# A hybrid decoder step: the sample's attention cut into nine pieces and laid between the prompt's attention steps, four state buffers, and the first part's recurrence laid between attention steps

## The reference

```python
n1 = rmsnorm(x, norm1_g); proj = n1 @ w_in          # q/k/v of both branches, gates
oa = banded_swa(qa, ka, va, sinks)                  # prompt: window 128, 16 heads, 4 kv heads
#  sample: one query per sequence against 127 cached keys and the new one (swa_sink_attend)
log_a = log_sigmoid(zb @ w_gla_gate + b) / 16
og, S_new = gla_recurrent(qg, kg, vg, log_a, S0)    # 4 heads, state 128 x 256 per head
og = rmsnorm(og, gla_norm_g) * silu(rb)
x = x + (sigmoid(ga) * oa + sigmoid(gb) * og) @ w_out
x = x + peer(rmsnorm(x, norm2_g))                   # below
...
def peer(h):   # per token: 8 heads x 16 picked experts of 16384
    ue = take(peer_u, eidx); act = gelu(ue . h); ve = take(peer_v, eidx)
    return sum(g * act * ve)
```

## Time and profile before

| | us |
|---|---|
| median of 3 runs (3849.88 to 3872.11) | 3852.84 |
| profiled execution, its own time | 3859.83 |
| its span in the trace | 3858.0 |
| PE busy | 2894.0 (75%) |
| DVE busy | 2808.5 (73%) |
| POOL busy | 2443.4 (63%) |
| ACT busy | 731.2 (19%) |
| first gather issued at | 484.80 |

### The profile page before, as it was taken

One profiled execution on the slowest core, in us unless ns is written; L12 is line 12 of the kernel. 1 busy time (PEld: TensorE's weight loads), 2 busy tenths in 40 slices (PEclk: granted clock), 3 DMA queues, 4 the chain that ended last, 5 costly groups with the idle time before them and its releaser, 6 DMA issues.

```text
span 3858.0 us, 33048 instructions
## 1 busy us (share of the span) xinstructions
PE 2894.0 (75%) x10008; PEld 1798.1 (47%) x10008; DVE 2808.5 (73%) x5630; ACT 731.2 (19%) x1677; POOL 2443.4 (63%) x2076
## 2 busy tenths in 40 slices
PE   8778689888687997887988768878777555555555
PEld 6667566456563665443664345545654111111111
DVE  0461797887788865866879897887879866667675
ACT  1321013332111131322111102322111110001001
POOL 0000077787667755765766777778667777777776
PEclk9889889899898997898999889989899777676677
DMA  4115399999999988898999999999999999999998
GB/s 149 54 36 183 110 376 407 350 356 396 420 403 345 405 331 324 306 328 309 396 402 375 326 363 403 401 328 370 421 411 380 338 371 368 363 377 385 367 400 336
DMA packets 342240, 1298.82 MB, mean 337 GB/s; under 512 B 39480, under 2 KB 48720, under 8 KB 321936
## 3 DMA queue, kind: packets, MB, share of 16 engines
q0 software_dynamic: 297216, 1082.26, 73.6%
q1 hardware_dynamic: 44848, 214.44, 14.3%
HBM read 1278.87 MB, written 19.76 MB: 337 GB/s over the span
## 4 chain that ended last, share of the span: by engine, by line
POOL 36%; PE 21%; DVE 14%; DMA 13%; issue 12%; DVEq 2%; ACT 0%; ACTq 0%; SPq 0%; POOLq 0%
POOL ringb L569 36%; DMA ringb<-in_v,eidx 9%; PE bank L834 8%; PE vsum L746 4%; DVE ringb L1294 4%; PE bank L1011 3%; DVE acc L1336 2%; PE bank L873 2%; PE bank L888 1%; DVE scT L1691 1%; PE bank L913 1%; DMA arena<-in_s 1%; DMA out_ss<-arena 1%; DMA ringb<-in_u,eidx 1%; DVE idx L1492 1%
## 5 line engine op out<-in xcount | busy, mean ns | idle before, releaser
L569 POOL DMA_INDIRECT ringb<-in_u,eidx x1024 | 1241.6, 1212 | 993.8 <-DVE eidx L1402 482.2
L746 PE MATMUL vsum<-ringb,diag 128*128 128x512 f32 x2160 | 1284.5, 737 | 646.6 <-DMA ringb<-in_v,eidx 603.8
L569 POOL DMA_INDIRECT ringb<-in_v,eidx x1024 | 1181.8, 1154 | 400.6 <-issue 300.1
L1294 DVE CUSTOM_DVE_ANT_0 ringb<-ringb,n2t 128x1024 f32<-128x1024 f32 x1032 | 1234.8, 1224 | 164.7 <-DMA ringb<-in_u,eidx 99.5
L746 PEld LDWEIGHTS vsum<-ringb,diag 128*128 128x128 f32 x2160 | 459.8, 228 | 1352.8 <-issue 1202.1
L1336 DVE SCALAR_TENSOR_TENSOR acc<-ringb,wgt,acc 128x1024 f32<-128x1024 f32 x484 | 622.3, 1286 | 326.0 <-DMA ringb<-in_v,eidx 313.7
L834 PE MATMUL bank<-wring,nTb 128*128 128x256 f32 x3024 | 683.4, 386 | 34.9 <-DMA wring<-in_w 31.1
L834 PEld LDWEIGHTS bank<-wring,nTb 128*128 128x128 f32 x3024 | 546.0, 182 | 175.5 <-DMA wring<-in_w 36.1
L1049 ACT ACTIVATE diag<-cst,wgt 128x128 f32<-128x128 f32 x540 | 206.9, 397 | 863.5 <-PE vsum L746 707.2
L873 PE MATMUL bank<-nTb,wring 128*128 128x256 f32 (+1 forms) x1152 | 264.0, 388 | 6.7 <-DMA wring<-in_w 4.1
L873 PEld LDWEIGHTS bank<-nTb,wring 128*128 128x128 f32 x1152 | 223.9, 195 | 60.6 <-issue 20.7
(11 more groups left out here) (231 smaller groups left out, 2212.5 us busy)
## 6 DMA issues: line engine op xcount, KB each, us to landing
wring<-in_w SPq DMA_DIRECT2D x152, 1024.0 KB, 7.8
ringb<-in_u,eidx POOLq DMA_INDIRECT x1024, 6.5
ringb<-in_v,eidx POOLq DMA_INDIRECT x1024, 6.6
n2t<-scratch_n SPq DMA_DIRECT2D x16, 512.0 KB, 7.4
oab<-in_xp SPq DMA_DIRECT2D x4, 1024.0 KB, 6.9
bTb<-in_keysT SPq DMA_DIRECT2D x4, 1024.0 KB, 9.1
vgb<-in_xp SPq DMA_DIRECT2D x4, 1024.0 KB, 8.9
scratch_h<-vgb SPq DMA_DIRECT2D x4, 1024.0 KB
```

Of the source, the lines that this page charges most:

```text
L569: pool.indirect_dma_start(out=ring[r], out_offset=None, in_=a["u"] if kind == "u" else a["v"], in_offset=bass.IndirectOffsetOnAxis(ap=at, ...
L746: last = mm(out[:, g * 512:(g + 1) * 512], lhs, ring[r][:, g * 512:(g + 1) * 512], start=(x == first), stop=(x == end))
L1294: v.tensor_tensor_reduce(out=ring[r], in0=ring[r], in1=n2t[:, n % 2, :], scale=1.0, scalar=0.0, op0=ALU.mult, op1=ALU.add, accum_out=dg[:, ...
```

## The change

Three things are changed.

First, part 0 takes its steps in another order (`mixer_order`): gate scores first, then attention steps with the recurrence's factors and units between them, and the four `ga` units at the end. For that the recurrence's buffers of part 0 move from `arena` into `ringb`, which no gather uses yet (`recurrence_room`).

Second, the sample's attention in part 2 becomes nine pieces (`sat`, 0 to 8), one after each attention step from 1 on; its evacuations count on a semaphore of their own (`sat`). Its scratch tiles move into `scT`, `kdTok` and `E0b`, and `vS` into `bTb`, where the cached keys are until the scores are made. So the values and the two window copies are issued after weight unit `vb` 3, once the scores are done, no longer after attention. The weights of the marks change: attention's points in part 2 weigh 13 for 10, and the four points of 16 each of the sample's attention are gone.

Third, the sample's states get four buffers (`S0 = 4`): SP issues four loads at once, and a buffer's store and reload follow three states later.

```diff
+def mixer_order(c):
+    NQ = 4 * CH[c]
+    at, A, B = [("at", n) for n in range(NQ + 2)], [("factors", n) ...], [("gla", n) ...]
+    if c == SC:
+        at = [at[0]] + [x for n in range(1, NQ + 2) for x in (at[n], ("sat", n - 1))]
+    if c or CH[c] != 2:
+        return at + [("between", 0), ("gate", 0), ("gate", 1)] + [x for pair in zip(A, B) for x in pair]
+    return [("gate", 0), at[0], at[1], ("gate", 1), at[2], A[0], at[3], B[0], at[4], A[1], at[5], B[1], at[6], A[2], at[7], B[2],
+            A[3], at[8], B[3], at[9]] + [("ga", u) for u in range(4)] + [("between", 0)]
...
-    out += [(("at", n, i), tokens(10) if i == 0 and n % CH[c] == 0 else 10) for n in range(4 * CH[c] + 2) for i in range(2)]
-    out += [(("sat", i), 16) for i in range(4)] if s else []
+    out += [(("at", n, i), (tokens(10) if i == 0 and n % CH[c] == 0 else 10) + 3 * s) for n in range(4 * CH[c] + 2) for i in range(2)]
...
+        def recurrence_room(c):
+            a0 = ringb if together(c) else arena
+            gates0 = 5 * D if together(c) else 0
...
-        SsT, Ps, PsT = (arena[:, 8 * CM + i * P:8 * CM + (i + 1) * P] for i in range(3))
+        SsT, Ps, PsT = scT[:, 0, :], kdTok[:, 0, :], E0b[:, 0:P]
-        vS = Pbb[:, :].rearrange("p (b c) -> p b c", b=NS)
+        vS = bTb[:, 0:2048].rearrange("p (b c) -> p b c", b=NS)
-        evac = {... for e in ("act", "dve")}
+        evac = {... for e in ("act", "dve", "sat")}
...
-                    if c == SC and (kind, u) == ("ga", 1):
-                        quads(MARKS[c][("sat", 0)])
+                    if c == SC and (kind, u) == ("vb", 3):
                         emptied(sp, ("va", c, 0, ST))
-                        sp.wait_ge(p_ready.sem, p_ready.at((c, 4 * CH[c] - 1)))
-                        sp.wait_ge(full.sem, full.at(("PT", c, 4 * CH[c] - 1, 1)))
+                        sp.wait_ge(full.sem, full.at(("sS",)))
                         sp.dma_start(vS[:, :, :], a["vcs"]).then_inc(d_vS, 16)
                         sp.wait_ge(d_vS, 16)
...
                         for b in range(NS):
-                            quads(MARKS[c][("sgla", b)])
-                            if b >= 2:
-                                sp.wait_ge(full.sem, full.at(("ogS", b - 2, 1)))
-                                sp.dma_start(o["ss"][b - 2]..., s0[b % 2]).then_inc(d_st[b % 2], 16)
-                                sp.wait_ge(d_st[b % 2], 16 * (b // 2))
-                            sp.dma_start(s0[b % 2], a["s0"][b]...).then_inc(d_s0[b % 2], 16)
+                            if b >= S0:
+                                quads(MARKS[c][("sgla", b - S0 + 1)])
+                                sp.wait_ge(full.sem, full.at(("ogS", b - S0, 1)))
+                                sp.dma_start(o["ss"][b - S0]..., s0[b % S0]).then_inc(d_st[b % S0], 16)
+                                sp.wait_ge(d_st[b % S0], 16 * (b // S0))
+                            sp.dma_start(s0[b % S0], a["s0"][b]...).then_inc(d_s0[b % S0], 16)
...
-        def pe_sample_attention(pe, beside):
+        def pe_sample_attention(pe, i):
+            if i == 0: # wait for the new keys; 64 score products (sS)
+            if i == 2: # turn SsT (sST)
+            if i == 4: # wait for the softmax; turn Ps (sPT)
+            if i == 6: # wait for vS; 64 products with the values (sO)
+            if i == 8: # 16 turns (sOt)
...
-                    if n == NQ - 1 and c == SC:
+                    if n == 0 and c == SC:
                         sample_operands()
+                    if n >= 2 and c == SC:
+                        dve_sample_attention(dve, n - 1)
                     beside("at", n, 1)
...
+                for what, n in mixer_order(c):
+                    if what == "at":
+                        attention(n)
+                    if what == "sat":
+                        pe_sample_attention(pe, n)
+                    if what == "between":
+                        between()
+                    if (what, n) == ("gate", 0):
+                        gate_scores()
+                    if what == "gla":
+                        recurrence(n)
+                    if what == "ga":
+                        unit(c, "ga", n)
```

More of the change, by code:

```diff
@@ L464, in build @@
         d_vS = sem("d_vS")
[L465 removed]
+        d_s0 = [sem(f"d_s0{i}") for i in range(S0)]
         d_keys = sem("d_keys")
@@ new lines, in pe_sample_attention @@
+            if i == 0:
+                pe.wait_ge(knew, 1)
+                ps = room(pe, ("sS",))
+                for half in range(2):
+                    lo = half * 64
+                    for b in range(NS):
+                        for Q in range(2):
+                            q = 2 * Q + half
+                            last = mm(ps[:, b * HA + q * 4:b * HA + q * 4 + 4], kTs[lo:lo + 64, Q, b, :], fmS[lo:lo + 64, 4 * Q:4 * Q + 4, b],
+                                      start=True, stop=True)
+                    if half == 0:
+                        pe.drain()
+                last.then_inc(full.sem, full.did(("sS",)))
@@ L878, in pe_program, with attention @@
                 emptied(pe, ("fm", c, 9))
-                for n in range(NQ + 2):
+                def attention(n):
                     beside("at", n, 0)
@@ new lines, in gate_scores @@
+                def gate_scores():
+                    beside("gate", 0)
+                    pe.wait_ge(d_par, 80)
+                    emptied(pe, ("fm", c, 18))
+                    for h in range(HB):
+                        ps = room(pe, ("gate", c, h))
+                        mm(ps[:, 0:CT], wg[:, h * DK:(h + 1) * DK], zbT[:, 0:CT], start=True, stop=True)\
+                            .then_inc(full.sem, full.did(("gate", c, h)))
+                    if c == SC:
+                        ps = room(pe, ("gateS",))
+                        for h in range(HB):
+                            last = mm(ps[:, h * NS:(h + 1) * NS], wg[:, h * DK:(h + 1) * DK], fmS[0:RANK, 18, :], start=True, stop=True)
+                        last.then_inc(full.sem, full.did(("gateS",)))
@@ L1207, in decays, with recurrence @@
                     act.sem_inc(e_ready.sem, e_ready.did((c, n)))
-                beside("gla", 0, 0)
-                decays(0)
-                for n, (h, t0, nt) in enumerate(units):
+                def recurrence(n):
+                    h, t0, nt = units[n]
+                    if n == 0 and not together(c):
+                        beside("gla", 0, 0)
+                        decays(0)
                     beside("gla", n, 2)
@@ L1226, in act_program @@
                         decays(n + 1)
-                    if ga_after(c, n) is not None:
+                    if ga_after(c, n) is not None and not together(c):
                         for p in pair_jobs(c):
                             sigmoid("ga", c, ga_after(c, n), p)
+                for what, n in mixer_order(c):
+                    if what == "at" and n <= NQ:
+                        attention(n)
+                    if (what, n) == ("sat", 3):
+                        sample_softmax()
+                    if (what, n) == ("gate", 0):
+                        gate_scores()
+                    if (what, n) == ("gate", 1) and together(c):
+                        decays(0)
+                    if what == "gla":
+                        recurrence(n)
+                    if what == "ga":
+                        for p in pair_jobs(c):
+                            sigmoid("ga", c, n, p)
                 if c == SC:
@@ L1703, in dve_program @@
                     beside("gla", n, 5)
+                for what, n in mixer_order(c):
+                    if what == "at":
+                        attention(n)
+                    if what == "between":
+                        between()
+                    if (what, n) == ("gate", 0):
+                        gate_scores()
+                    if (what, n) == ("gate", 1):
+                        cumulate()
+                    if what == "factors":
+                        factors(n)
+                    if what == "gla":
+                        recurrence(n)
+                    if what == "ga":
+                        branch_gate(n)
                 if c == NCH - 1:
```

393 lines of the change are left out of this document (195 added, 198 removed).

## The result

The changed kernel took 3805.61 us (median of 4 runs, 3796.31 to 3816.66) beside 3862.48 for the kernel before (4 runs, 3849.88 to 3881.05): ratio 0.9884, 95% interval 0.9844 to 0.9925, faster by 29 to 60 us. The forecast was 3809, that is 44 us off the 3852.84 that the kernel before had then. The profiled execution of the changed kernel took 3796.31 itself, the lowest of its four, span 3794.4, 63.6 less than the span before.

What follows compares the result with a forecast made beforehand. From about 482 us the DMA engines' gathers bound the kernel, before that part 0's chain through the mixer. Savings of 17 + 20 + 7 = 44 us took 3859.8 to 3815.8, and 7.0 lower on the median's scale to 3809; range 3790 to 3835.

Steps and rivals of the forecast that it cites:

- Part 0: Part 0's new order of the same instructions: 25.6 us saved, less 9 for the low clock, about 17.
- where before `rb` begins at 279: End of part 0 in the kernel before, set against 253.4 in the new order: 25.6 us saved.
- The 9 us charged for the clock: Part 0: PE's low clock behind waits for DVE's sums, 3 us for each of three cycles.
- The sample's attention: Part 2's attention with the sample's attention in pieces: stretch of 181 us becomes 161, 20 saved.
- Both needs close to it will not dovetail perfectly, and I take 161: Part 2's attention stretch: PE needs 144 us, the DMA engines 157 at best; 161 taken.
- a DMA share of 0.95 and no wait of PE over 6 us: Expected sign in part 2, from attention's first step to the gate scores, with a length of about 161 us.
- The states: The sample's states with four loads in flight: 7 us saved, bounds 0 and 8.
- at 0.98 it is 83: The sample's states: DMA engines' need of 91 x 0.89 = 81 us becomes 83 at a share of 0.98.
- PE as the bound in part 2's attention (3824): Rival for part 2's attention: the stretch takes 176 us and saves 5, total 3824 us; chance 0.18.
- The low clock through part 0: Rival for part 0's new order: 10 us lost there, 27 kept from part 2, 3836 us; chance 0.08.
- The slower case: Rival: low clock in part 2's attention, mean below about 0.75, 20 us slower, 3873 us; chance 0.04.
- if the clock drops in either interleaved stretch: Sign that the forecast is wrong: PE's clock drops in part 0's new order or part 2's attention with the pieces.

Runs made afterwards that it cites:

- the second run with late copies: The changed kernel with part 0's first `ga` unit ahead of its last recurrence unit and the window copies at the second `wo` unit: 3861.27 us, 0.9968 beside the changed kernel.

## Why the prediction was right

The time came 3.4 us below the forecast, and the gain of 44 is what three timings show (45, 50 and 42 by their ratios). The two terms that the runs can resolve, part 0 and the buffers, are there. But the sizes of the terms were off both ways and made each other good: that the sum came out is in part luck.

**Part 0**: forecast 17, measured 24.3 (23.3 in the run that undoes it). The schedule was right: `ga` was to start at 225 + 9 = 234 and starts at 234.42. The step that failed is "where before `rb` begins at 279": the row of PE that starts at 278.74 has 288 products, nine units, and its first is the last `ga` unit; `rb` begins at 286, 7 us later. So the gain is 286 less 262.3 (234.4 + 27.8), 24. The 9 us charged for the clock came in sum, and that is luck, for they were not where I put them: 5.6 are in the head, where the first masks start at 139.9 for 134.3; two cycles take 31.0 and 30.5 for 30.1; and about 3 are in the tail, where the scores of the last unit stand behind the wait of 8.41 at the lower clock. In the head only a part is a wait's (again S takes 3.78 behind a wait of 2.27, as in the earlier trace rows); the gate scores begin at 96.87, not 95, and the first `vb` unit takes 8.86 for 7.17 with no wait before it. The forecast "3 us for each of three cycles" was refuted: behind the wait the products lose about 1.2 us a cycle, and S and the `vb` unit nothing. Here the Trainium skill, "TensorE: Matmul & The Clock Gate", section "HAM oscillation — how this bites in real kernels", has short bursts between waits start cold every time. With that the trace agrees: the products right behind each wait are slow (1.19 for 0.59). That "every cycle would be paid at the low clock" went beyond that, and it did not come: S and the unit 5 us later are at the upper clock (1.99, 7.17).

**The sample's attention**: forecast 20, the stretch gained 13.6, and by the run that undoes the pieces 7 are kept at the end in the mean, with an interval from -4 to 19: the 20 is refuted, a gain is not shown. Two steps failed. "Both needs close to it will not dovetail perfectly, and I take 161" left out that the copies now stand in the middle of attention: "part of the delay hides" was too hopeful, since a gather of 17.38 us stopped PE for 5.33 (9.30 before) and put the next 13 us at the lower clock; without them the stretch is 162, and 164.5 in the second run with late copies. And the term took a shorter stretch for time won, though one quad had left it. The need of PE, 144, was right (144.0 and 147.8 in the two runs with late copies). The sign "a DMA share of 0.95 and no wait of PE over 6 us" was half met: 0.89, and 5.33.

**The states**: forecast 7 with bounds 0 and 8, measured 19.7 in the stage; the run with two buffers puts the buffers at 11.7 in the stage and 11 to 29 us in the time. The other 6 (96.2 before, 90.3 in that run) lie between single executions; their cause stays open. The step that failed is "at 0.98 it is 83": it reckoned the DMA engines' need by their busy share, and took the mean share of a long stretch for a ceiling. The same rows give it by bytes: 91 us at 316 GB/s are 28.8 MB, and at the 378 GB/s of the last of the earlier trace rows they take 76 us. In this stage the share is now 1.01 and the rate 380 GB/s, before 0.89 and 319: each busy us moved fewer bytes before, so the share alone understated what was left. The window was short too, 91 us for a stage of 96.2. That the loads in flight, not SP's wait for the stores, set the pace was right in kind, and the stage's 90.3, 84.9 and 76.5 to 78.6 us with two, three and four buffers show it step by step.

**Rivals.** PE as the bound in part 2's attention (3824) is half true: PE was busy 154.8 of 169 us, and the stretch took between the forecast's 161 and that rival's 176; and the cause was the late `v` tile behind the copies, which that rival had named. The low clock through part 0 did not come (0.85 in the mean). The slower case needed a mean clock below 0.75 in the stretch; it was 0.86. That "a gain of part 2 comes back as DMA idle time in the recurrence behind it" did not come either: that stage took 174.4 for 174.8, with one quad more in it. One sign of a wrong forecast did come: "if the clock drops in either interleaved stretch". It dropped in both, behind the waits of part 0 and twice in part 2, at the 64 score products and behind the copies, where the kernel before had 0.97 up to 1480. So the time was met although a condition of the reasoning was not.

## What to carry to other kernels

Before a stage's length is compared, count the gathered work in it: where marks shift work between stages, a stage can be 16 us shorter because four quads have left it, which says nothing of the kernel's time. A large copy that nothing waits for belongs where the engine that it delays has slack. Work added to test an idle engine must end before the wait does, or it hides what it should show. And an average share over a long stretch is no ceiling for a short one (bytes over the best rate seen come nearer), nor is the start of a row of products that of its last group: read the count of the row.

## What the runs showed of the hardware

The clock fell while TensorE was never idle. The windows of the changed kernel around the 64 score products (64x4 each, from 1360.83 without a gap):

```profile
1362.00:1364.00 2.00, 2.00 (x18) 2.00 (x19) 1.87 (x5) 1.95 (x3) 1.70 (x2) 0.93 0.93 363
1364.00:1376.00 12.00, 11.92 (x43) 9.75 (x44) 5.47 (x8) 4.39 (x13) 4.24 (x4) 0.50 0.72 289
```

The first 24 took 0.9 us for each eight, all later ones 1.7 to 1.8, with the sums of gathered tiles behind them at 6.23 for 3.65. It is the same in all twelve traces with the pieces: the clock falls 1.7 to 4.9 us behind the start of this row. In the kernel before, which has the same attention step there without the row, the clock is 1.00 up to 1378, falls only behind a wait of 5.04 us, and is 1.00 again from 1400 to 1480. So it is likely the long row of tiny products that brings the lower clock, much as waiting does; it is not proven, since PE also waited 1.36 to 2.57 us some 5 us ahead of the row in each of the twelve, and nothing was tried that would spread the row. Between the two halves PE stopped for 4.07 to 6.12 us in nine of these traces (5.44 in the second execution of the changed kernel, below), with no releaser in the profile ("issue"), and hardly or not at all in the trace shown and in the two with the marks of before; the cause stays open.

```profile
1387.51 6.98 PE L793 MATMUL bank<-fmS,bTb 64*128 64x4 f32 x32 [5.44 <-issue]
```
